# Norms summed on VectorE ahead of TensorE, and three waits of the expert stage moved, in a two-block kernel on one Trainium2 core

## What is computed

```python
def _rmsnorm(x, g):
    xf = x.astype(jnp.float32)
    y = xf * lax.rsqrt(jnp.mean(xf * xf, axis=-1, keepdims=True) + EPS) * g.astype(jnp.float32)
    return y.astype(x.dtype)
...
def layer_norm(x, g, b):
    xf = x.astype(jnp.float32)
    mu = jnp.mean(xf, -1, keepdims=True)
    var = jnp.mean(jnp.square(xf - mu), -1, keepdims=True)
    return ((xf - mu) * lax.rsqrt(var + LN_EPS) * g.astype(jnp.float32) + b.astype(jnp.float32)).astype(x.dtype)
...
def moe_ffn(u, w_router, w13, w2):
    ...
    for e in range(N_EXPERTS):
        gate_e = jnp.sum(jnp.where(top_idx == e, top_w, 0.0), axis=-1).astype(t.dtype)
        out = out + gate_e[:, None] * swiglu(t, w13[e], w2[e])
    return out.reshape(Bsz, S, D)
```

## Time and profile before

| what | value |
|---|---|
| median of three runs | 3569.03 us |
| profiled execution, its own time | 3570.84 us |
| its span, first to last instruction | 3569.0 us |
| mean granted TensorE clock | 0.951 |
| TensorE busy | 91% of the span |
| VectorE, ScalarE busy | 27%, 13% |
| bytes read by DMA, mean rate | 729.32 MB, 206 GB/s |

### The profile page before, as it was taken

One profiled execution on the slowest core, in us unless ns is written; L12 is line 12 of the kernel. 1 busy time (PEld: TensorE's weight loads), 2 busy tenths in 40 slices (PEclk: granted clock), 3 DMA queues, 4 the chain that ended last, 5 costly groups with the idle time before them and its releaser, 6 DMA issues.

```text
span 3569.0 us, 56279 instructions
## 1 busy us (share of the span) xinstructions
PE 3238.4 (91%) x24190; PEld 2724.6 (76%) x24191; DVE 966.9 (27%) x2010; ACT 473.6 (13%) x1075; POOL 15.0 (0%) x26
## 2 busy tenths in 40 slices
PE   4999999899899999989998888999579999999997
PEld 3888888788788888877887777788567876678874
DVE  5203221231130221323103423448631111111112
ACT  1001022110000101111000200002511111001110
POOL 0000000000000000000000000000000000000000
PEclk7999999899999999999999968999789999999999
DMA  8645543265374464325535503681228788898884
GB/s 331 245 177 194 220 144 117 87 246 192 128 261 169 182 236 154 112 94 211 222 145 214 190 0 119 245 303 54 78 84 327 302 315 310 308 359 324 319 316 171
DMA packets 55183, 732.17 MB, mean 205 GB/s; under 512 B 6577, under 2 KB 6761, under 8 KB 10517
## 3 DMA queue, kind: packets, MB, share of 16 engines
q1 hardware_dynamic: 51092, 716.69, 53.2%
q0 software_dynamic: 3968, 13.74, 1.1%
HBM read 729.32 MB, written 4.23 MB: 206 GB/s over the span
## 4 chain that ended last, share of the span: by engine, by line
PE 79%; DMA 9%; DVE 8%; issue 2%; ACT 1%; DVEq 0%; SPq 0%; POOL 0%; ACTq 0%; POOLq 0%
PE psum L618 48%; PE psum L1017 11%; PE psum L1057 9%; DMA ring<-in_up_dram 3%; DVE ring L1385 2%; DMA ring<-in_up_e_dram 2%; PE psum L668 2%; DMA ring<-in_w_qk_dram 1%; PE psum L796 1%; PE psum L1034 1%; PE psum L1073 1%; DVE work L1815 1%; DVE rms L1443 0%; PE psum L680 0%; PE psum L635 0%
## 5 line engine op out<-in xcount | busy, mean ns | idle before, releaser
L618 PE MATMUL psum<-h_t,ring 128*128 128x256 f32 x6336 | 1397.3, 383 | 113.8 <-ACT h_t L1143 67.2
L618 PEld LDWEIGHTS psum<-h_t,ring 128*128 128x128 f32 x6336 | 1214.5, 192 | 296.5 <-issue 122.5
L618 PE MATMUL psum<-work,ring 128*128 128x256 f32 x2752 | 611.4, 386 | 27.5 <-ACT work L1216 6.8
L618 PEld LDWEIGHTS psum<-work,ring 128*128 128x128 f32 x2752 | 532.4, 194 | 105.7 <-issue 17.8
L1017 PE MATMUL psum<-h_t,ring 128*64 128x96 f32 x11264 | 468.8, 246 | 7.7 <-DMA ring<-in_up_e_dram 6.1
L1017 PEld LDWEIGHTS psum<-h_t,ring 128*64 128x64 f32 x11264 | 465.4, 137 | 11.1 <-issue 11.0
L1057 PE MATMUL psum<-ring,work 128*96 128x512 f32 x704 | 304.0, 593 | 7.7 <-DVE work L2105 6.6
L1385 DVE SCALAR_TENSOR_TENSOR ring<-ring,cond 128x1024 f32<-128x1024 f32 x240 | 279.3, 1220 | 25.6 <-DMA ring<-in_ada_dram 17.4
L1057 PEld LDWEIGHTS psum<-ring,work 128*96 128x96 f32 x704 | 114.2, 163 | 192.1 <-issue 187.5
L1420 DVE TENSOR_TENSOR work<-work,psum 128x256 f32 (+1 forms) x126 | 53.1, 421 | 675.7 <-PE psum L618 660.8
L2105 DVE TENSOR_TENSOR work<-work,psum 128x256 f32 x176 | 74.1, 421 | 401.2 <-PE psum L1017 401.2
(11 more groups left out here) (305 smaller groups left out, 1557.8 us busy)
## 6 DMA issues: line engine op xcount, KB each, us to landing
ring<-in_up_e_dram SPq DMA_DIRECT2D x64, 2048.0 KB, 7.6
ring<-in_ada_dram SPq DMA_DIRECT2D x60, 2048.0 KB, 8.2
ring<-in_up_dram SPq DMA_DIRECT2D x55, 2048.0 KB, 8.9
ring<-in_down_e_dram SPq DMA_DIRECT2D x32, 1792.0 KB, 8.1
ring<-in_down_dram SPq DMA_DIRECT2D x20, 2816.0 KB, 9.6
ring<-in_up_e_dram SPq DMA_DIRECT2D x32, 1536.0 KB, 8.2
ring<-in_down_e_dram SPq DMA_DIRECT2D x16, 2048.0 KB, 7.8
ring<-in_w_qk_dram SPq DMA_DIRECT2D x12, 2048.0 KB, 9.1
```

Of the source, the lines that this page charges most:

```text
L618: mm = pe.matmul(half(b), w, moving(k, j * lin.groups + m), start=(k == 0), stop=(k == depth - 1))
```

## The change

- `norm`: VectorE adds the squares of tiles 1 to 6 into tile 0 of h, each when ScalarE has made it (`squares_so_far`, called in `add_to_x` ahead of the next tile's add). TensorE multiplies tile 0 by ones, then tile 7: two products for eight.
- norm0 of the first layer: VectorE makes the six additions after the sum of the first condition chunks.
- ln0 and ln1 (`ln_after`): VectorE sums x into `rms` (`x_so_far`), and TensorE multiplies `rms` and then tile 7.
- ln2 and ln3 (`ln_along`): still eight products, each behind its own add to x. The second sum of a layer norm, over squares, keeps its eight products.
- Gather: the gates' transposes come first, in bank 7 instead of 5; their copy is VectorE's first. The up products wait for each tile of h singly, inside the first group of each round.
- Down: banks of the last three groups of up are awaited at the third part of the first side, except bank 0, which down writes first.

```diff
+    norm = with_(uses(b5=1), squares=DT, most_squares=1, root=1, scaled=DT, h=DT)
     ln = with_(uses(b5=1, b6=1), mean=DT, squares=DT, root=1, h=DT)
+    ln_after = with_(ln, most_x=1)
+    ln_along = with_(ln, x_summed=DT)
...
+        def gathered(f):
+            b = LIN + f % LIN
+            return b, f // LIN + (1 if b == BANKS - 1 else 0)
...
             def norm(p):
                 pe.wait_ge(bank_free[5], reads(p, 5))
-                for k in range(DT):
-                    pe.wait_ge(signal["squares"], p.of("squares", k + 1))
-                    mm = pe.matmul(half(5), ones[:, :], h[:, k, :], start=(k == 0), stop=(k == DT - 1))
-                mm.then_inc(signal["full5"], 1)
+                pe.wait_ge(signal["most_squares"], p.of("most_squares", 1))
+                pe.matmul(half(5), ones[:, :], h[:, 0, :], start=True, stop=False)
+                pe.wait_ge(signal["squares"], p.of("squares", DT))
+                pe.matmul(half(5), ones[:, :], h[:, DT - 1, :], start=False, stop=True).then_inc(signal["full5"], 1)
+
+            def mean(p):
+                pe.wait_ge(bank_free[5], reads(p, 5))
+                if "most_x" in p.what:
+                    pe.wait_ge(signal["most_x"], p.of("most_x", 1))
+                    pe.matmul(half(5), ones[:, :], rms[:, :], start=True, stop=False)
+                    for b in range(LIN):
+                        pe.wait_ge(bank_free[b], reads(p, b))
+                    pe.matmul(half(5), ones[:, :], x[:, DT - 1, :], start=False, stop=True).then_inc(signal["full5"], 1)
+                else:
...
+                    for k in range(DT):
+                        pe.wait_ge(signal["x_summed"], p.of("x_summed", k + 1))
+                        mm = pe.matmul(half(5), ones[:, :], x[:, k, :], start=(k == 0), stop=(k == DT - 1))
...
             def up_rounds(p, gp, width):
...
                             for k in range(lin.depth):
+                                if c == 0 and m == 0:
+                                    fb, use = gathered(k)
+                                    pe.wait_ge(bank_free[fb], reads(gp, fb, use) + 1)
...
                 down = p.what
+                late = plan.stage["upE"].at[-1][-3:]
                 for b in range(LIN):
-                    pe.wait_ge(bank_free[b], reads(p, b))
+                    if b not in [bank_of for _, bank_of, _, _ in late] or b < lists:
+                        pe.wait_ge(bank_free[b], reads(p, b))
                 for side in range(2):
                     for part, (first, last) in enumerate(zip(down.edges, down.edges[1:])):
                         slot = chunk_landed(p.slot(side * down.parts + part))
+                        if side == 0 and part == down.parts - 1:
+                            for _, b, _, _ in late:
+                                pe.wait_ge(bank_free[b], reads(p, b))
...
+            def squares_so_far(p, f):
+                dve.wait_ge(signal["squares"], p.of("squares", f + 1))
+                e = dve.tensor_tensor(h[:, 0, :], h[:, 0, :], h[:, f, :], ALU.add)
+                if f == DT - 2:
+                    e.then_inc(signal["most_squares"], 1)
+                else:
+                    e.then_inc(dve_done, steps.one())
+                    dve.wait_ge(dve_done, steps.count())
...
-            def add_to_x(p, scale):
+            def add_to_x(p, scale, after):
...
+                        if f > 1 and "most_squares" in after.what:
+                            squares_so_far(after, f - 1)
+                        elif f > 1:
+                            for k in range(LIN):
+                                dve.wait_ge(bank_free[k], reads(after, k) - 2 + (k < f) + (k + 4 < f))
+                            x_so_far(after, f - 1)
...
             ada_next(p, 0, ada_b(0))
+            for f in range(1, DT - 1):
+                squares_so_far(place("norm0", 0), f)
```

More of the change, by code:

```diff
@@ L1655, in _ @@
                 ada_next(on("up2"), 0, ada_b(3, l))
-                add_to_x(on("down2"), gate)
+                add_to_x(on("down2"), gate, place("norm0", at(l, 1, 1)))
             p = place("final_norm")
@@ L1912, in _ @@
                 b = down.what.at[j][m][0]
+                if f > 1:
+                    for k in range(LIN):
+                        dve.wait_ge(bank_free[k], reads(place("ln1"), k) - 2 + (k < f) + (k + 4 < f))
+                    x_so_far(place("ln1"), f - 1)
                 dve.wait_ge(*group_end(down, j, m, 0, down.slot(j)))
```

81 lines of the change are left out of this document (37 added, 44 removed).

## The result

The changed kernel took 3537.41 us, the median of six runs (3532.02 to 3542.45). The kernel before took 3562.43 us in six runs (3555.8 to 3577.43), the three shown before among them. The ratio is 0.9926, 95% interval [0.9903, 0.9949], so 26 us less, between 18 and 35. The forecast was 3540, range 3527 to 3557. The profiled execution took 3542.45 us, span 3540.7, granted clock 0.947 (before: 0.951).

What follows compares the result with a forecast made beforehand. TensorE was taken to bound the kernel, with 79% of the chain that ended last. Terms -8.35 + 3.0 - 3.1 - 10.5 - 5.2 - 5.2 gave -29.4 us, median 3540 us, range 3527 to 3557.

Steps and rivals of the forecast that it cites:

- Norms, -8.35: norm1 and norm2 of both layers and final_norm: two products for eight let the root start 1.67 us earlier at each.
- the first rival: Stands behind norms, ln0, ln2, ln3: fewer busy rows lower TensorE's clock, 11.8 us back, 3552 us; chance 0.10.
- First norm, +3.0: First layer's norm0: six additions behind VectorE's last condition sum cost 3.0 us more, bounds 1.5 and 4.
- Norm0 of the second layer, 0: Norm at the layer loop's restart: no gain, since the dropped products were hidden under VectorE's 6 us.
- ln0, -3.1: Sum over x behind the last add at ln0: 14 of 16 rows go, 3.1 us less.
- ln1, 0: At ln1: no gain, VectorE ends last and its six additions lie between down products.
- ln2, -5.8: At ln2: products start behind their own adds, 5.8 us less; 3.0 less at the low clock.
- ln3, -4.7: At ln3: products start behind their own adds, sum ends 4.7 us earlier; low end 1.5.
- Gather, -5.2: Eight experts' up products start 0.65 us earlier each behind the gather, waits per tile free; bounds nothing and 8.8.
- Down, -5.2: Before the experts' down products: 5.2 of 6.6 us waiting for VectorE go; bounds 2 and 6.6.
- Experts' gain lost to DMA: Expert stage: bound by DMA, gather and down gains become waits on the ring, 10.4 us back, 3550; chance 0.10.
- Code that doesn't fit: Experts' loop-backs: TensorE's longer code overflows its store, 8.0 us at each of six, 3588 us; chance 0.04.

Runs made afterwards that it cites:

- experiment 2: Kernel before with the layer-norm change alone (ln0 and ln1 summed on VectorE, ln2 and ln3 product by product): 3561.0 us, ratio 0.9975.
- experiment 3: Kernel before with the change to the gather alone: 3565.13 us, ratio 0.9989.
- experiment 4: Kernel before with the change to the down projection alone: 3564.62 us, ratio 0.9989.
- experiment 5: Kernel before with every load of expert weights cut to its first half, same count of products: 3558.3 us, ratio 0.9964.
- experiment 1: Kernel before with the change to the norms alone, including the first norm's six additions: 3558.87 us, ratio 0.9975.
- experiment 6: Changed kernel with every load of expert weights cut to its first half: 3523.83 us, ratio 0.9871.
- experiment 7: Changed kernel with halved expert loads, waits for h gathered: four banks before each round's first product. One execution, 3538.59 us.
- experiment 10: Changed kernel with 14 products of ones by ones, read by nobody, behind the two products of every norm: 3530.55 us, ratio 0.9891.
- experiment 8: Kernel before with six small copies added on VectorE ahead of the first condition sum: one execution, 3568.36 us.
- experiment 9: Kernel before with 24 small copies on VectorE ahead of the first condition sum: 3568.3 against 3568.12 us, ratio 0.9996.
- experiment 11: Changed kernel with the first norm's six additions moved ahead of VectorE's first condition sum: 3543.67 us, ratio 0.993.

## Why the prediction was right, and where it was not

**Norms, -8.35: the mechanism and the size are right**, 5 x 1.67 exactly. What the sum left out is the first rival, which was in part true: over the five norms the 64th row starts 2.4 us later in sum in the five kernels with the change (without fillers) than in the seven without it (15.4 becomes 16.4 at both norm2s). I had priced it as all or nothing at 11.8 us and a chance of 0.10; it is 2.4 on average, with sums over the five norms of 79.4 to 82.4 us against 76.5 to 78.8. The stand behind the norm kept its length (3.90 and 3.97 us); what the change took away are rows ahead of it.

**First norm, +3.0: mis-sized, +0.8.** VectorE's path from the last condition sum to the mean square did grow by 3.07 us (54.30 to 59.41, before 56.06 to 58.10). The step that failed is the one from there to the first product: it started at 61.7 to 63.3 us in five kernels without the additions on this path (before, experiments 2 to 5) and at 62.9 to 64.0 in five with them (after, experiments 1, 6, 7 and 10), 0.8 later on average. Without the additions the product stood 1.1 to 2.3 us behind the first tile of h, for its weights, and with them 0.05 (0.5 in the kernel with fillers). So from the last condition sum to the product it grew by 1.7 us, not by 3.07. The other 0.9 us are no effect that I can name: the condition sums ended that much earlier in the five with them. I had not asked which wait ends last there.

**Norm0 of the second layer, 0: wrong, -4.5.** I took VectorE's 6 us as given. They were two stands at a loop-back, and the second belonged to a boundary between blocks of code, which twelve more instructions ahead of the loop (six additions, six waits) moved out of its way. The gap fell from 12.3 to 13.4 us to 8.2 to 8.5, 4.5 less on average. It was luck of position, as experiments 8, 9 and 11 show.

**ln0, -3.1: right** (18.5 to 15.36 us between products). **ln1, 0: right.** **ln2, -5.8:** 17.3 to 17.7 us from the last product to the reciprocal (16.0 in one kernel) became 11.8 in five kernels and 13.5 in two, the changed kernel's own profile being one of these (-4.2). The chosen end of the estimate occurs more often, the low one (-3.0) not at all. **ln3, -4.7: right** (15.7 to 11.07).

**Gather, -5.2: too large; -1.2 with halved loads, -3.4 with whole ones.** Three steps failed. Up starts 1.0 us earlier, not 0.65, but in six experts of eight. The waits per tile cost 0.34 us per expert, not 0: the rows inside a round's first group do spread, the sign that I had named myself. And the copy of the gates, which I had put at no delay, makes up start 1.5 us later in the first expert.

**Down, -5.2: right, low.** -8.2 with halved loads, -6.7 in the profile. I had taken 5.2 of the 6.6 us in seven experts and left out the eighth's 1.0 and the overlap with up's tail, 0.07 each; a late first slice cost 1.4 us in two experts, not 0.1 to 0.5 in each. The wait is gone in six of eight. So the two parts of the expert stage come to 10.1 us together for a forecast of 10.4, because their errors nearly cancel.

**Experts' gain lost to DMA: no.** The profiles of before and after, taken alone, seemed to say so (7.7 us of 10.4); half loads and the four profiles on each side give 9.4 and 10.1, counted from the transposes.

**Code that doesn't fit: not by this change.** One costly loop-back in the kernel after, as before. The rival's mechanism is real, since it struck once in a kernel with the old body, at 9.25 us against 8.0.

Put together with what was measured: -8.35 + 2.4 + 0.8 - 4.5 - 3.1 - 5.8 - 4.6 - 10.1 = -33.3, or -31.6 with ln2 as profiled. The two spans differ by 28.3 us, the medians by 25 and by the ratio 26. The sum lies inside the interval's far end (-35). With halved loads the medians of the two kernels differ by 34 us.

Most of the distance to the two spans is the draw of the two profiles. With the values of this pair alone (first product +0.3, norm0 of the second layer -4.8, 64 rows behind the seven norms +5.2, ln2 -4.2, expert stage -7.3) the same sum comes to -27. So the forecast of -29.4 is close by partly cancelling errors: gains that it did not see (4.5 at norm0 of the second layer, 2.2 at the first norm) against a loss that it did not see (2.4 of clock), and a gather priced too high against a down priced too low.

## What to carry to other kernels

Ask at each step which wait ends last: six additions on VectorE's path took 3.1 us there and moved the product behind them by 1.7, since its weights were due 1 to 2 us behind h. Put waits that are almost always fulfilled ahead of one product each, not in a bunch at a loop's start. Where the clock drops behind a stand of TensorE, cover the stand with products that nobody reads, up to its end. Where a stage streams its weights, cut the loads in half to see a change of a few us; two single profiles differ by as much without any change.

## What the runs showed of the hardware

- A stand of TensorE of 4 us or more at a norm costs its own length and, in the kernel after, 2 to 3 us more: 64 rows behind a norm start within 15.7 to 16.7 us there, within 13.7 where fillers cover the stand, and within 16.4 and 16.5 where they end 3.4 and 3.8 us too early. It is no fixed price: in the kernel before, one such stand of 3.90 us cost nothing (13.67 us). The Trainium skill (TensorE: Matmul & The Clock Gate, Why this matters for your kernels) asks for short gaps between bursts; the rows with fillers agree.
- VectorE's restart of a loop of 900 us stood 3 us for code (2.9 to 3.6), and another 4.0 to 4.7 us where a block boundary fell within the loop's first operations; 8.67 us in one stand where it lay just ahead of them. The Trainium skill (Runtime: NRT & Kernel Launch, Instruction fetch mechanics) says that a taken branch to code outside the loaded pages stalls for a fetch. The rows agree, and show besides that the stand can come in two parts.
- Four register waits that are long fulfilled, bunched ahead of a loop body's first product, cost TensorE 0.36 us per pass, eight of them spread over eight products 0.10.
- The same expert code took 474.9 to 479.3 us for its up products in five profiles (before, experiments 1, 2, 8 and 9), and 466.4 with half the bytes.
